# Expert weights in pairs of slots, expert activation turned by VectorE, rotation, row numbers and token rows rearranged

## The reference

```python
def moe_swiglu(h, router_w, router_b, w_gate, w_up, w_down):
    logits = (t @ router_w) + router_b
    top_vals, top_idx = lax.top_k(logits, TOP_K)            # 2 of 8
    gates = jax.nn.softmax(top_vals, axis=-1)
    combine = jnp.sum(one_hot(top_idx) * gates[..., None], axis=1)
    for e in range(N_EXPERTS):
        out = out + combine[:, e:e + 1] * swiglu(t, w_gate[e], w_up[e], w_down[e])

def swiglu(h, w_gate, w_up, w_down):                        # hidden width 1408
    return (jax.nn.silu(h @ w_gate) * (h @ w_up)) @ w_down
```

## Time and profile before

| what | value |
|---|---|
| median of 3 runs | 1320.54 us |
| profiled execution, its own time | 1319.2 us |
| its span, first to last instruction | 1317.6 us, granted clock 0.992 |
| TensorE (PE) busy | 97% of the span |
| VectorE (DVE) / ScalarE (ACT) / POOL busy | 48% / 22% / 5% |
| moved by DMA | 368.72 MB, mean 280 GB/s |

### The profile page before, as it was taken

How to read it: one execution, slowest core, us unless ns; L and a number is a source line. 1 busy time by engine, 2 the same in 40 slices (tenths; PEclk the granted TensorE clock), 3 DMA queues, 4 the chain that set the end, 5 groups by cost and what they waited for, 6 DMA issues and landing times.

```text
span 1317.6 us, 27465 instructions
## 1 busy us (share of the span) xinstructions
PE 1275.1 (97%) x10876; PEld 967.6 (73%) x10876; DVE 635.6 (48%) x1602; ACT 292.7 (22%) x772; POOL 71.0 (5%) x126
## 2 busy tenths in 40 slices
PE   6999999999999999999999998999989999999997
PEld 4768888999999767799999986778555455445545
DVE  5465464888887625457676764762610000000003
ACT  4332203212112414520000031264211011101103
POOL 0100000000000000000000001000010000000020
PEclk9999999999999999999999998999999999999998
DMA  9999783677776662237767776402999999999990
GB/s 348 413 401 403 262 298 125 213 282 271 266 276 236 254 214 80 97 113 267 288 254 286 278 285 232 168 1 97 383 411 409 410 410 410 410 410 410 410 378 32
DMA packets 92391, 368.72 MB, mean 280 GB/s; under 512 B 10243, under 2 KB 10499, under 8 KB 83930
## 3 DMA queue, kind: packets, MB, share of 16 engines
q1 hardware_dynamic: 75026, 271.29, 54.6%
q0 software_dynamic: 17296, 96.50, 18.9%
HBM read 347.69 MB, written 20.05 MB: 279 GB/s over the span
## 4 chain that ended last, share of the span: by engine, by line
PE 88%; DVE 4%; DMA 3%; issue 2%; ACT 2%; SPq 1%; POOL 0%; ACTq 0%; DVEq 0%; POOLq 0%
PE banks L941 20%; PE banks L666 15%; PE banks L928 11%; PE banks L1265 11%; PE banks L1316 8%; PE banks L1287 4%; PE banks L691 4%; PE banks L786 2%; PE banks L1008 2%; PE banks L746 2%; PE banks L857 1%; PE banks L841 1%; DMA ring<-stream 1%; DMA side<-ada 1%; DVE side L1728 1%
## 5 line engine op out<-in xcount | busy, mean ns | idle before, releaser
L1728 DVE CUSTOM_DVE_ANT_0 side<-side 128x1024 f32<-128x1024 f32 x128 | 151.0, 1220 | 33.6 <-DMA side<-ada 33.4
L1265 PE MATMUL banks<-ring,arena 128*32 128x512 f32 x1536 | 166.3, 592 | 0.0
L928 PE MATMUL banks<-arena,ring 128*128 128x256 f32 x704 | 160.2, 380 | 0.0
L666 PE MATMUL banks<-h,ring 128*128 128x256 f32 x640 | 145.8, 386 | 6.4 <-DVE arena L1798 5.6
L2292 DVE TENSOR_TENSOR arena<-arena,banks 128x256 f32<-128x256 f32 (+1 forms) x48 | 14.7, 334 | 284.4 <-ACT arena L1657 284.4
L928 PEld LDWEIGHTS banks<-arena,ring 128*128 128x128 f32 x704 | 130.2, 190 | 17.2 <-issue 1.4
L666 PEld LDWEIGHTS banks<-h,ring 128*128 128x128 f32 x640 | 121.6, 192 | 28.8 <-DVE arena L1798 5.7
L1265 PEld LDWEIGHTS banks<-ring,arena 128*32 128x32 f32 x1536 | 50.0, 110 | 111.2 <-issue 110.1
L666 PE MATMUL banks<-arena,ring 128*128 128x256 f32 x384 | 84.6, 380 | 2.6 <-DVE arena L2013 2.1
L941 PEld LDWEIGHTS banks<-h,ring 128*128 128x128 f32 x672 | 81.5, 192 | 2.1
L666 PEld LDWEIGHTS banks<-arena,ring 128*128 128x128 f32 x384 | 72.5, 190 | 13.3 <-DVE arena L2013 2.9
(11 more groups left out here) (333 smaller groups left out, 1587.1 us busy)
## 6 DMA issues: line engine op xcount, KB each, us to landing
ring<-stream SPq DMA_DIRECT2D x247, 512.0 KB, 5.5
ring<-experts SPq DMA_DIRECT2D x192, 512.0 KB, 15.7
side<-ada POOLq DMA_DIRECT2D x64, 1024.0 KB, 7.6
side<-experts SPq DMA_DIRECT2D x48, 512.0 KB, 17.2
arena<-experts SPq DMA_DIRECT2D x24, 512.0 KB, 16.7
yrows<-side POOLq DMA_DIRECT2D x1, 6144.0 KB, 32.6
hrows<-side POOLq DMA_DIRECT2D x1, 5632.0 KB, 17.8
logit<-hrows POOLq DMA_DIRECT2D x8, 512.0 KB, 7.1
```

The source lines that it names most:

```text
L666: last = pe.matmul(bank(u, a, a + T), ring[:, s, (k0 + kc) * P:(k0 + kc + 1) * P], moving[:, kc, :], start=(kc == 0), stop=(kc == kn - 1))
L928: last = pe.matmul(banks[:, 4 + c // 2, (c % 2) * T:(c % 2 + 1) * T], ring[:, s, c * P:(c + 1) * P], hid[:, j % 2, :], start=False, stop=F ...
L1265: ins = pe.matmul(banks[BLOCK * j:BLOCK * (j + 1), t, :], hg[:, k, BLOCK * t:BLOCK * (t + 1)], ring[:, m, (j % 2) * 512:(j % 2 + 1) * 512] ...
L1728: dve.tensor_tensor_reduce(weights, weights, cond[:, 0 if layer0 else 1, :], 1.0, 0.0, ALU.mult, ALU.add, accum_out=msum[:, n:n + 1]).then ...
```

## The change

- Expert weights: the slots 0 to 31 are loaded in pairs, one transfer of 1 MB (8 KB per partition) for two neighbouring slots, when both are empty; slot 32 comes alone from an array of its own. 17 transfers per expert instead of 33. Consumers wait on the pair.
- The activation is turned by VectorE's transpose (within blocks of 32 x 32) right after each block is made, three of 256 and three of 96 columns per pass; the down matrix is ordered by blocks of 32 rows to suit. TensorE's nine transposes, their two ScalarE and one VectorE copies out of PSUM and the three small moves are gone.
- Pass 0: the row transposes come after the whole of `expert_down`. Only 96 rows are loaded per expert.
- `brow` is no longer computed by TensorE and copied by ScalarE: POOL writes the shift to DRAM and loads it back to all partitions after `norm(4)`, and POOL, not VectorE, adds it to the token rows, after the gather has read them.
- Routing on VectorE: the slot numbers, then the row numbers, then the extra passes. POOL scatters after the row numbers.
- `oo`: six router blocks after chunk 6; after chunk 7 token chunks 0 and 2, the column sums, the last two router blocks, token chunks 1 and 3.
- Indexer: `rope(5)` first, then ada unit 5, `rope(6)`, unit 6, `rope(7)`, unit 7, `rope(8)`, modulation, `rope(9)`, then the shift row's two operations.
- First block: ada units 11 and 12 move from the branch loop into the attention; the loop keeps three.

```diff
+        def moe_pair(m):
+            n = 2 if m < MSLOTS - 1 else 1
+            if m >= TAIL:
+                return arena[:, (m - TAIL) * SLOT:(m - TAIL + n) * SLOT]
+            tile, at = (ring, m) if m < RING else (side, m - RING)
+            return tile[:, at:at + n, :].rearrange("p a n -> p (a n)")
+
...
-            for m in range(MSLOTS):
+                if m == MSLOTS - 1:
+                    return lasts[bass.ds(expert, 1)].rearrange("a p n -> p (a n)")
+                return experts[bass.ds(expert * (MSLOTS // 2) + m // 2, 1)].rearrange("a p n -> p (a n)")
+
+            for m in range(0, MSLOTS, 2):
                 if m < RING:
                     sp.wait_ge(slot_used[m], before[m])
+                    sp.wait_ge(slot_used[m + 1], before[m + 1])
                 elif m == RING:
                     sp.wait_ge(s_mod, 9)
-                    sp.wait_ge(nought_out, 32)
+                    sp.wait_ge(nought_out, 64)
                 elif m == TAIL:
                     sp.wait_ge(s_o, 20)
                     sp.wait_ge(U["oo", 7].done[0], U["oo", 7].done[1])
-                sp.dma_start(moe_slot(m), experts[m]).then_inc(slot_full[m], 16)
+                sp.dma_start(moe_pair(m), lasts[0] if m == MSLOTS - 1 else experts[m // 2]).then_inc(slot_full[m], 16)
             with sp.Fori(1, EXPERTS - 1) as p:
-                for m in range(MSLOTS):
-                    sp.wait_ge(*emptied(m, p))
-                    sp.dma_start(moe_slot(m), weights(m, p)).then_inc(slot_full[m], 16)
-            sp.wait_ge(s_routed, 1)
+                for m in range(0, MSLOTS, 2):
+                    sp.wait_ge(*emptied(min(m + 1, MSLOTS - 1), p))
...
             pool.wait_ge(s_mod, 9)
             pool.wait_ge(s_h, 40)
+            third, at = norm_scale_source(5)[0]
+            pool.dma_start(shift_row.rearrange("(p c) -> p c", p=P), mod[:, third, at:at + 8]).then_inc(nought_out, 16)
+            pool.wait_ge(nought_out, 16)
+            pool.dma_start(brow, shift_row.rearrange("(o n) -> o n", o=1).broadcast_to([P, D])).then_inc(nought_out, 16)
             pool.memset(nought, 0.0).then_inc(consts_set, 1)
             pool.wait_ge(consts_set, 4)
             for rows in (hrows.rearrange("(r e) n -> r e n", r=P), yrows.rearrange("e t s q n -> (e t s) (q n)").rearrange("(r e) n -> r e n", r=P)):
                 pool.dma_start(rows, nought.rearrange("p (o n) -> p o n", o=1).broadcast_to([P, rows.shape[1], D])).then_inc(nought_out, 16)
-            pool.wait_ge(nought_out, 32)
-            pool.wait_ge(s_routed, 2)
+            pool.wait_ge(nought_out, 64)
+            pool.wait_ge(s_gather, 2)
+            for tile in range(2):
+                rows = htok[:, tile, :].rearrange("t (c p) -> t c p", c=KC)
+                pool.tensor_tensor(rows, rows, brow.rearrange("t (p c) -> t c p", c=KC), ALU.add).then_inc(consts_set, 1)
+            pool.wait_ge(consts_set, 6)
+            pool.wait_ge(s_routed, 1)
             for k in range(4):
                 pool.indirect_dma_start(hrows, bass.IndirectOffsetOnAxis(ap=target[:, k:k + 1], axis=0),
                                         htok[:, k // 2, :], None).then_inc(rows_stored, 16)
             pool.wait_ge(rows_stored, 64)
-            pool.dma_start(hgtok, hrows[CAP:CAP + P, :]).then_inc(rows_in, 16)
+            pool.dma_start(hgtok[0:CAP, :], hrows[CAP:2 * CAP, :]).then_inc(rows_in, 16)
             pool.wait_ge(s_passes, 1)
...
                 pool.wait_ge(rows_stored, 64 * (p + 1))
                 pool.wait_ge(s_hgt, p)
-                pool.dma_start(hgtok, hrows[bass.ds((p + 1) * CAP, P), :]).then_inc(rows_in, 16)
+                pool.dma_start(hgtok[0:CAP, :], hrows[bass.ds((p + 1) * CAP, CAP), :]).then_inc(rows_in, 16)
             where = yrows.rearrange("e t s q n -> (e t s) (q n)")
...
                     if r == 5 and c == 6:
-                        for k in range(4):
+                        for k in range(6):
                             router_block(k)
-                if r == 5:
-                    router_block(4)
-                    router_block(5)
-                    norm_sum(r)
-                    router_block(6)
-                    router_block(7)
             def router_block(k):
...
-                token_chunks(t)
-            third, at = norm_scale_source(5)[0]
-            pe.wait_ge(s_std, 6)
-            pe.wait_ge(s_route, 4)
-            for c in range(KC):
-                last = pe.matmul(banks[:, U["brow"].bank + c // 4, (c % 4) * P:(c % 4 + 1) * P],
-                                 mod[:, third, at + c:at + c + 1].broadcast_to([P, P]), ident,
-                                 start=(c % 4 == 0), stop=(c % 4 == 3), skip_group_check=True)
-            last.then_inc(aux_done, 1)
+            token_chunks(0)
+            token_chunks(2)
+            norm_sum(5)
+            router_block(6)
+            router_block(7)
+            token_chunks(1)
+            token_chunks(3)
             u = U["ranks"]
             begin(u)
...
-
-                count = 3 if c == 2 else QUADS
-                for j in range(count):
-                    m = DOWN_SLOT[c] + j
-                    pe.wait_ge(slot_full[m], 16 * (before[m] + p + 1))
-                    final = c == 2 and j == count - 1
+            def expert_down(p, first, last):
+
+                for c in range(first, last):
+                    m = DOWN_SLOT + c
+                    pe.wait_ge(slot_full[m - m % 2], 16 * (before[m - m % 2] + p + 1))
+                    final = c == DOWN - 1
                     for t in range(BLOCKS):
+                        if c == 0:
+                            pe.wait_ge(s_hidT, HIDS * p + t + 1)
+                        if c == WIDE // BLOCK:
+                            pe.wait_ge(s_hidT, HIDS * p + BLOCKS + t + 1)
                         for q in range(QUADS):
                             ins = pe.matmul(banks[BLOCK * q:BLOCK * (q + 1), 6 + t // 2, (t % 2) * T:(t % 2 + 1) * T],
-                                            mhidT[:, c, t, BLOCK * j:BLOCK * (j + 1)], moe_slot(m)[:, T * q:T * (q + 1)],
-                                            start=(c == 0 and j == 0 and t != 1), stop=final, skip_group_check=True)
+                                            mhidT[:, t, BLOCK * c:BLOCK * (c + 1)], moe_slot(m)[:, T * q:T * (q + 1)],
+                                            start=(c == 0 and t != 1), stop=final, skip_group_check=True)
                             if final:
                                 ins.then_inc(s_down, 1)
...
                 if not first:
                     pe.wait_ge(s_hid, HIDS * p + BLOCKS)
                     row_transposes(p)
-                pe.wait_ge(s_hid, HIDS * p + 5)
-                hidden_transposes(0, 4)
-                pe.wait_ge(s_hid, HIDS * p + 6)
-                hidden_transposes(1, 5)
-                hidden_transposes(2, 3)
                 if not first:
                     pe.wait_ge(s_y, 2 * p)
-                pe.wait_ge(s_hidT_act, 5 * p + 1)
-                expert_down(p, 0)
+                expert_down(p, 0, WIDE // BLOCK)
                 if first:
                     pe.wait_ge(s_cpick, 2)
                     pick_transposes(0, 2)
-                pe.wait_ge(s_hidT_dve, p + 1)
-                expert_down(p, 1)
+                expert_down(p, WIDE // BLOCK, DOWN)
                 if first:
                     pick_transposes(1, 4)
                     row_transposes(p)
-                pe.wait_ge(s_hidT_act, 5 * p + 5)
-                expert_down(p, 2)
             expert_pass(0, True)
...
-            for t in range(4):
+            for t in (0, 2, 1, 3):
                 u = U["htok", t]
                 act.wait_ge(*u.done)
                 act.activation(htok[:, t // 2, (t % 2) * 512:(t % 2 + 1) * 512], bank(u), ACT.Copy,
             act.wait_ge(s_route, 12)
             lg = rt[:, 112:128]
             act.activation(lg, lg, ACT.Exp).then_inc(s_gexp, 1)
-            act.wait_ge(*U["brow"].done)
-            for half in range(2):
-                act.activation(brow[:, half * 512:(half + 1) * 512], banks[:, U["brow"].bank + half, :], ACT.Copy).then_inc(s_h, 1)
...
                 silu(0, WIDE)
                 silu(1, NARROW)
-                act.wait_ge(s_hidtr, 3 * p + 1)
-                act.activation(mhidT[:, 0].rearrange("p a n -> p (a n)"), banks[:, 4, 0:BLOCKS * P], ACT.Copy).then_inc(s_hidT_act, 1)
-                act.wait_ge(s_hidtr, 3 * p + 3)
-                mixed = banks[:, 3, 0:BLOCKS * P].rearrange("p (t n) -> p t n", t=BLOCKS)
-                act.activation(mhidT[0:NARROW, 2, :, 0:NARROW], mixed[0:NARROW, :, 0:NARROW], ACT.Copy).then_inc(s_hidT_act, 1)
-                for a in range(3):
-                    rows = slice(BLOCK * a, BLOCK * (a + 1))
-                    act.activation(mhidT[NARROW:P, 2, :, rows], mixed[rows, :, NARROW:P], ACT.Copy).then_inc(s_hidT_act, 1)
                 if first:
                     act.wait_ge(s_picktr, 1)
...
```

(40 more changed lines are left out.)

56 lines of the change are left out of this document (23 added, 33 removed).

## The result

The changed kernel takes **1305.79 us** (median of 5 runs, 1303.07 to 1310.03), the kernel before 1317.74 in the same five rounds (1317.01 to 1320.67): a ratio of 0.9912, 95% interval 0.9888 to 0.9936. It is faster by 12.0 us, about half of the 23.5 that I forecast; 1305.8 lies at the far end of the range. The profiled execution is the slowest of the five: 1310.03 us, span 1308.4, 9.2 less than the profiled one of before. So between the two profiles 14.3 us of the forecast are missing, and they can be read off place by place.

A forecast was written before the change was run, and what follows sets the result against it. TensorE, busy 97% of the span, bounds the kernel; 7.6 + 2.1 + 2.4 + 4.5 + 6.9 = 23.5 us off 1319.2 gives 1295.7, with the median 1.3 above: 1297 us. Own range 1293 to 1302, with rivals 1291 to 1306.

The forecast's parts named there:

- The passes from the fourth on: Seven passes after pass 0: each loses 0.98 us of TensorE transposes, 6.9 us gained in all, period 43.6 us.
- VectorE's transposes: Expert passes: three of 256 and three of 96 columns, from nothing to 1.2 us each, costing TensorE nothing.
- The branches: End of the first block's branches: TensorE's waits of 1.17 and 0.94 us go, gain 2.1 us, bounds 0 and 2.3.
- The indexer's stop: Indexer: TensorE's 5.63 us idle and 2.2 us of halved clock go, gain 7.6 us, bounds 4 and 8.
- The weights: Expert weight loads stay hidden: 1.8 us reserve at the old rate, 12 us more with 8 KB rows 3.8% faster.
- Rival 1: Last passes: 8 KB rows are no faster, the weights become the bound and TensorE waits; 1301 us, chance 0.12.
- Rival 3: Every pass: the row round trip doubles to 33 us beside 8 KB rows, 4.6 us wait each; 1329 us, chance 0.04.
- pass 0: First expert pass: TensorE's 3.27 us wait for rows and its activation transposes go, gain 4.5 us, bounds 2 and 5.
- the routing: Last `oo` unit to the ranks: gain 2.4 us; 2.7 if the clock stays up, 1.9 or 0 if it falls.
- Rival 2: Front half: a late ada load moves the stop, the clock drops again, 5 to 8 us return; 1304 us, chance 0.08.

## Why the prediction was half right

*What held.* The passes from the fourth on: 43.59 us each as said. VectorE's transposes, which had no row, take 0.44 or less for 256 columns and 0.27 for 96, in the lower half of my bounds, and wait for nobody. The branches: 2.1 forecast, 2.5 found. The indexer's stop: 7.6 forecast, 7.7 found up to the first score. The weights: TensorE never waits for them in the changed kernel. I had given 8 KB rows 25.9 GB/s per engine from the earlier trace rows; beside full queues they go at 78.41 MB / (0.962 x 16 x 200 us) = 25.5, by this row:

```profile
q1 hardware_dynamic: 11129, 78.41, 96.2%
```

In the run with 4 KB rows it is 77.61 MB / (0.981 x 16 x 200 us) = 24.7, so pairs are 3% faster. The reserve was smaller than I said, but there. Rival 1 was near: with 4 KB rows TensorE waits 5.7 us, and with 23 us gained 1.57 even with pairs. Rival 3 did not come: the row load of pass 1 is issued 992.59 - 981.79 = 10.8 us after the start, 10.3 before. The Trainium skill, DMA: Bandwidth & Descriptors, section Queues, rings and completion order, has an engine drain a packet of some 9 to 17 descriptors before it turns to the next queue. The wait for the scatters here (11.87 and 11.47 beside 4 KB rows, 16.40 beside 8 KB) grew by about what I had worked out for one larger row in between for each of theirs, 5 us. Turns of several rows from either queue would give the same growth, so no run here shows how long a turn is, and my reading of the rule, several weight rows for one of POOL's, did not come about.

*The step that failed first: pass 0.* "Between nothing and, say, four times VectorE's 1.18 each (9.4) they stay hidden" asked only whether POOL was done in time, 5.7 us against 11.8, and it was. It did not ask what a POOL addition does to VectorE beside it. The two copies of the table stood still until POOL had finished, 4.8 us, so the row numbers came at 16.5 instead of 11.8. The scatters' 4.5 us more I had counted, but not that the row load would take longer to land beside the larger rows (8.9 and 9.7 us, 7.7 before). So the rows were there 47.6 us after the start instead of 42 (48.4 in the second profile), and TensorE had asked at 45.7 (44.0). The term of 4.5 us came to 0.3, and to -0.5 in the second profile. Taking the additions off POOL and off the path gave it back: pass 0 in 45.33 against the 45.6 forecast. The Trainium skill, SBUF — State Buffer, section Who interferes with whom, has the rule that I should have weighed here: VectorE and GpSimd share a pair of ports, a VectorE copy in a two-port mode takes it, and the one that comes second is blocked until the other's instruction ends. The trace agrees to the tenth of a us, with the ends at 935.07 and 937.89 against 935.03 and 937.86; that it is this port no run here shows, only that POOL's additions do it.

*The second: the clock.* I counted 2.2 us of the indexer for a clock that would no longer fall, and the routing at 1.9 to 2.7 with a fall of the old length. Between 800 and 990 us the changed kernel's two profiles have 24 us at half clock, the kernel before 10. Place by place between the first pair of profiles: 3.8 us lost at the scores and the values unit; 4.5 in the routing, where the term of +2.4 came to -2.1. Up to the ranks it came as forecast: they begin 4.7 us after the last `oo` unit, not 7.9, less 0.9 for the two router blocks ahead of it, 2.3. Then the ranks took 1.1 longer and the gather 3.3, both at half clock. And 3.2 in pass 1, whose 46.76 should have been 43.6; with the clock up it takes 44.15 (run with the additions ahead), so 2.6 of it is the clock. With the 4.2 of pass 0 and 0.2 of the third pass this is 15.9; the part up to the scores brought 0.8 more than forecast and the last norm 0.7, which leaves 14.4 for the 14.3 missing. The bounds that I had set, 4 for the indexer and 0 for the routing, did not look one stretch further on. Nor was the range 1293 to 1302 what they give: the lower bounds add up to 12.9, and 1319.2 - 12.9 + 1.3 is 1307.6.

Rival 2 named this outcome, "the clock drops again", but for another reason, a load that came late, and none came late. In the routing the filled versions ran at 1.00 in all four profiles and every other profile has a half stretch there, which shows that it is the feeding of TensorE. At the scores the three filled or interleaved profiles ran at 1.00 as well, but that shows less: of the eight with the changed kernel's order and nothing put between, six have a half stretch there, of 3.4 or 6.8 us, and two have none. So there it is a chance, not a fixed price. What decides between them stays open.

With these two mended the gain comes to the forecast: with the additions ahead it is 19.9 us over before in the same rounds, still with 6.8 us at half in the routing, and with that filled 23.2, where I had forecast 23.5. That the figures meet so closely is in part luck: the profile of that kernel still has 6.8 us at half, at the scores and the out projections, that I had not counted, and filling the routing was no part of the change.

## What to carry to other kernels

Before work is moved to POOL because it is idle, read which VectorE instructions will run beside it, their small copies too: the question is not only when POOL is done, but whom it holds up until then. A stop of TensorE that is taken away pays its idle time, but its share of lost clock may come due in the next thin stretch; look at the granted clock there, and fill waits of about a microsecond with a few idle products where the products cost no more than the wait. And a transfer that arrives just too late costs its wait and the clock after it, so a reserve of 2 us on a chain with two unknown terms is none.
